# Smaller modulation transfers sent one by one, V's mix moved into an earlier call, and reordered seams, in a two-network transformer kernel

## The chip, the cores and the metric

The kernel runs on one core of a Trainium2 chip. The metric is the device time of one execution in microseconds (us). Before the change three runs took 2808.93 us in the median (2806.24 to 2821.59).

## The reference

The reference computes two networks on 256 rows of 1024 numbers, all in float32. Both have two layers.

```python
def first_block(x, ...):
    for layer in range(2):
        x = x + 0.5 * swiglu_ffn(rms_norm(x, ffn1_norm[layer]), w_gu, w_down)   # 1024 -> 2816 -> 1024
        p = rms_norm(x, mix_norm[layer]) @ w_in            # two gates, u_a, v_a, and r, k, v, low-rank parts
        y_a = chunked_sgu(u_a, v_a, ...)
        y_b, v_first = rwkv7_time_mix(token_shift_mix(p_b, mu), v_first, ...)
        x = x + (sigmoid(gate_a) * (y_a @ w_a) + sigmoid(gate_b) * (y_b @ w_b)) @ w_out
        x = x + 0.5 * swiglu_ffn(rms_norm(x, ffn2_norm[layer]), ...)
    return rms_norm(x, final_norm)

# inside rwkv7_time_mix, in the second layer alone:
v = v + (v_first - v) * sigmoid(v0 + v_res_down @ v2)

def second_block(x, c, ctx, ...):
    for i in range(2):
        sh1, sc1, g1, sh2, sc2, g2 = split(silu(c) @ ada_w[i] + ada_b[i], 6)    # "modulation"
        y = attention(rmsnorm(x) * (1 + sc1) + sh1, ctx ...)
        x = x + g1 * y
        x = x + g2 * conv_ffn(rmsnorm(x) * (1 + sc2) + sh2, ...)  # the context alike, in layer 0 only
    return rmsnorm(x, norm_out)
```

## The kernel before

**Weights.** All large weights come as one stream of 371 units of 1 MB each (128 rows of 2048 float32), in the order of use. SyncE sends unit u into `raw[u % 2]`. ScalarE copies it in a rounded type to `w_hi` (L1072), VectorE computes the rest `w_lo = raw - w_hi` (L1575), and both lie in 4 slots. A slot of `raw` is free for SyncE when `w_lo` is done, a slot of `w_hi`/`w_lo` when TensorE has used it (`unit_done`). The helper `split(n)` on ScalarE and on VectorE does this for the next n units, at places written by hand. Each product is three matmuls (`w_hi` by the feature's high part, `w_lo` by it, `w_hi` by the feature's low part), 24 for a unit.

**Engines.** Each engine has its own program, in order, and they meet in semaphores. `Side` keeps the counts. A normalised feature is made so: TensorE transposes X into a bank of PSUM (`raw_half`, `normed_features`), VectorE scales it to `TF`, ScalarE copies `TF` to `HA_hi`, VectorE forms `HA_lo`. In the first network this needs no norm, as the rows' rates are applied to the product later (`raw_features`). In the second (`modulated`) the rates come first: squares and a square root on ScalarE, a diagonal matrix on VectorE (`DIAG`), a matmul that spreads it over the partitions, then `TF`.

**The first network's mixer.** After 14 units (`pb`) come low-rank products, and then `wkv(l, g, t)` four times in each layer: `wkv_parallel` builds products of keys and inverts 64x64 triangles in five levels (`TM` on VectorE, two matmul groups, `XX` on ScalarE), and `wkv_chain` carries the state over two chunks. TensorE's instructions here are thousands of 64x64 matmuls, written out without a loop.

**Modulation.** The 24 MB of `ada_w` of each layer are brought in 24 units during this stage into `ADW`, which has 8 slots on the memory of `w_hi` and `w_lo`. SyncE sends unit n as soon as slot n-8 has been used (`ada_used`, L404). TensorE uses four units at each of the four calls, the first eight ahead of them (`mod_units`). Behind these 24 issues in SyncE's queue stands the next unit of the weight stream (L387). In layer 1 the two slots of `raw` hold `VF` and `VSIG` for V's mix, so the stream also waits for `v_ready`.

**V's mix** (`v_residual(t)`, layer 1): three VectorE instructions for rows t=0 ahead of the calls, and three for t=1 at the start of the second call, (g, t) = (0, 1).

**Seams.** A seam is a place where one stage's end must be normalised before the next stage can start: `mixer_residual` and `ffn_residual` with `raw_features` in the first network, `attend` and `conv_ffn` in the second, and the last norm and output. `down()` multiplies by the down-projection with both pairs of PSUM banks, `ACC[0]` and `ACC[1]`.

Of the kernel before, what the change touches and what calls it, by code (L numbers as in the profile page):

```python
# [131 lines left out]
PB_END = [PLAN[f"gate_a{l}"][0] for l in range(2)]  # L132

# [53 lines left out]
def build(nc, wstream, wada, vecs, cols, consts, x_in, ctx_in, mus, lora, lort, wst, convw, cc, lam,  # L187
          toe, rope, window, out, mod_scr, vfirst_scr):
    ctx = ExitStack()
    with ctx:  # L190
# [189 lines left out]
        def _(eng):  # L380
            for u in range(RAW):
                eng.dma_start(raw[:, u, :], wstream[u]).then_inc(sem[f"land{u}"], 16)
# [14 lines left out]

            def modulation(l):
# [14 lines left out]
            eng.wait_ge(sem["out_ready"], 1)  # L413
            eng.dma_start(out.rearrange("a (t p) d -> p (a t) d", p=P), XN[:, :, :]).then_inc(sem["out_land"], 16)
            eng.wait_ge(sem["out_land"], 16)
# [3 lines left out]
        def _(pe):  # L419
# [245 lines left out]
            def mod_units(l, a, b):  # L665

                for n in range(a, b):
                    group, k = divmod(n, 8)
                    bank = MOD_BANK[group]
                    pe.wait_ge(sem[f"ada_land{n % ADA_SLOTS}"], c.next(f"ada_land{n % ADA_SLOTS}", 16))  # L670
# [266 lines left out]
            def attend():  # L937
# [14 lines left out]
                for j in range(2):  # L952
                    block_wide(HA_hi, HA_lo)

            def conv_ffn(l, s):
                if l:
                    normed_features(X, 0)
# [30 lines left out]
            for l in range(2):  # L988
                project(l)
                if l:  # L990
                    attend()
                    phase()
# [4 lines left out]
            phase()  # L997
# [58 lines left out]
        def _(act):  # L1056
# [26 lines left out]

            def root(n, dst=None, at=0):
# [55 lines left out]
            def swiglu(first=False, last=False):  # L1140
                raw_features(0 if first else 1)
# [306 lines left out]
            def attend():  # L1448
# [26 lines left out]
                for j in range(2):  # L1475
                    e.skip(2, 1)
                    split(2)

            def conv_ffn(l, s):
                if l:  # L1480
                    row_squares(0)
                    modulated(1, 1, 0)
                else:
# [53 lines left out]

            act.wait_ge(sem["const_land"], c.next("const_land", 32))
            split(2)
# [7 lines left out]
            for l in range(2):  # L1547
                project(l)
                if l:
                    attend()  # L1550
                    phase()
# [4 lines left out]
            phase()  # L1556
            squares(X, XN)
# [3 lines left out]
        def _(dve):  # L1561
# [89 lines left out]
            def raw_features(gain, residual=None):  # L1651

                for h in range(2):
                    if residual:
                        residual(h)
                    raw_half(gain, h)
                if residual:
                    split(2)
                dve.wait_ge(sem["ss_ready"], c.next("ss_ready"))
# [52 lines left out]
            def mixer_residual(n):  # L1712

                x = cols(X, n)
                dve.wait_ge(sem["unit_done"], e.reached())
# [3 lines left out]
                if n == 0:  # L1719
                    split(2)  # L1720
# [32 lines left out]
            def v_residual(t):  # L1753

                tt(VF[:, t, :], VF[:, t, :], V[:, t, :], ALU.subtract)
                dve.drain()
                tt(VF[:, t, :], VF[:, t, :], VSIG[:, t, :], ALU.mult)
                dve.drain()
                tt(V[:, t, :], V[:, t, :], VF[:, t, :], ALU.add)
                dve.drain()  # L1760
# [786 lines left out]
```

## Time and profile before

| | |
|---|---|
| profiled execution | 2815.72 us, span 2813.8 us |
| TensorE (PE) busy | 2641.3 us, 94% of the span |
| weight loads (PEld) | 2113.4 us, 75% |
| VectorE (DVE) / ScalarE (ACT) | 1691.4 us, 60% / 1399.0 us, 50% |
| DMA | 477.80 MB, mean 170 GB/s |
| granted clock of TensorE | 0.971 of full speed, mean |

Busy time of TensorE is modelled and can hide short stops; the chain of work that ended last tells more. In a row, `L430` is the helper of all matmuls, `L506` that of the transposes, "issue" is time in which an engine waited for nothing that the profile shows. `SPq` is SyncE's queue.

### The profile page before, as it was taken

Reading aid. Unit: us, or ns where it says so; the run is one execution under the profiler, and the core shown is the slowest. Engines: PE = TensorE matmul, PEld = TensorE weight load, DVE = VectorE, ACT = ScalarE, POOL = GpSimd, SP = SyncE. Lnnn points to the kernel's source line nnn. Section 1 sums busy time; section 2 is a strip of 40 time slices with the busy share of each in tenths; the row PEclk is TensorE's granted clock in tenths of the full one; section 3 lists DMA queues with packets and bytes.
Section 4 is the critical chain, followed back from the end, with each engine's and each line's share of the span. In section 5 each row is a group of like instructions: output and inputs, shape, how many; then the busy total and the mean of one; then the engine's idle time right before and its main releaser. Section 6 shows DMA issues by size and latency. Waiting matters only on the chain.

```text
span 2813.8 us, 45474 instructions
## 1 busy us (share of the span) xinstructions
PE 2641.3 (94%) x18123; PEld 2113.4 (75%) x18123; DVE 1691.4 (60%) x1882; ACT 1399.0 (50%) x1679; POOL 78.3 (3%) x109
## 2 busy tenths in 40 slices
PE   6999888999999999888999999988999999997998
PEld 5877576887878877567878887757888887866886
DVE  4545735765545546646755555677776776455574
ACT  4435333644434434334536444474775764455573
POOL 0001000000000001000000000000000000010000
PEclk9999998999999999999999999999999999988999
DMA  4556922444454458532554544403544454523343
GB/s 186 193 187 234 369 81 85 170 175 179 179 194 178 181 186 291 232 127 99 195 190 179 195 174 155 165 1 115 196 177 175 175 193 163 190 88 125 120 179 120
DMA packets 73419, 477.80 MB, mean 170 GB/s; under 512 B 8830, under 2 KB 13020, under 8 KB 18864
## 3 DMA queue, kind: packets, MB, share of 16 engines
q1 hardware_dynamic: 60608, 440.43, 41.9%
q0 software_dynamic: 8048, 30.93, 3.1%
q10 hardware_dynamic: 4608, 4.20, 0.6%
q8 instruction: 120, 1.97, 0.3%
q14 instruction: 35, 0.29, 0.0%
HBM read 466.83 MB, written 2.13 MB: 167 GB/s over the span
## 4 chain that ended last, share of the span: by engine, by line
PE 81%; DVE 7%; DMA 4%; ACT 4%; issue 2%; DVEq 1%; ACTq 0%; POOL 0%; SPq 0%; POOLq 0%
PE ACC L430 72%; PE TP L506 3%; PE MM L430 3%; DMA raw<-wstream 3%; DVE w_lo L1575 2%; PE TP L430 2%; ACT w_hi L1072 1%; DMA ADW<-wada 1%; DVE ST L2060 1%; PE TP L882 1%; ACT XX L1214 1%; DMA BIAS<-toe 0%; DVE PR L2072 0%; DMA COL<-cols 0%; ACT U L1228 0%
## 5 line engine op out<-in xcount | busy, mean ns | idle before, releaser
L1575 DVE TENSOR_TENSOR w_lo<-raw,w_hi 128x2048 fp32r<-128x2048 f32 x371 | 842.0, 2290 | 383.6 <-ACT w_hi L1072 360.9
L1072 ACT ACTIVATE w_hi<-raw 128x2048 fp32r<-128x2048 f32 x371 | 703.9, 1916 | 413.4 <-DMA raw<-wstream 271.8
L430 PE MATMUL ACC<-w_hi,HA_hi 128*128 128x512 f32 (+1 forms) x2032 | 807.3, 397 | 31.8 <-DVE HA_lo L1647 13.9
L430 PE MATMUL ACC<-w_hi,HA_lo 128*128 128x512 f32 (+1 forms) x2032 | 796.0, 392 | 0.0
L430 PE MATMUL ACC<-w_lo,HA_hi 128*128 128x512 f32 (+1 forms) x2032 | 796.0, 392 | 0.0
L430 PEld LDWEIGHTS ACC<-w_hi,HA_hi 128*128 128x128 f32 x2032 | 387.8, 191 | 115.9 <-issue 25.9
L430 PEld LDWEIGHTS ACC<-w_hi,HA_lo 128*128 128x128 f32 x2032 | 387.3, 191 | 81.1
L430 PEld LDWEIGHTS ACC<-w_lo,HA_hi 128*128 128x128 f32 x2032 | 388.2, 191 | 76.5
L430 PE MATMUL ACC<-w_hi,FT_hi 128*128 128x512 f32 x616 | 246.0, 399 | 7.0 <-issue 7.0
L430 PE MATMUL ACC<-w_hi,FT_lo 128*128 128x512 f32 x616 | 244.2, 396 | 0.0
L430 PE MATMUL ACC<-w_lo,FT_hi 128*128 128x512 f32 x616 | 244.1, 396 | 0.0
L1149 ACT ACTIVATE HID<-ACC,ST 128x256 f32<-128x256 f32 x88 | 37.0, 471 | 221.7 <-PE ACC L430 221.7
L430 PEld LDWEIGHTS ACC<-w_hi,FT_hi 128*128 128x128 f32 x616 | 116.0, 188 | 35.6 <-issue 8.4
L1674 DVE SCALAR_TENSOR_TENSOR HID<-ACC,ST,HID 128x256 f32<-128x256 f32 x88 | 38.6, 480 | 168.1 <-ACT HID L1149 168.1
L430 PEld LDWEIGHTS ACC<-w_hi,FT_lo 128*128 128x128 f32 x616 | 116.0, 188 | 28.2
L430 PEld LDWEIGHTS ACC<-w_lo,FT_hi 128*128 128x128 f32 x616 | 116.1, 188 | 27.3
L430 PE MATMUL ACC<-w_hi,HB_hi 128*128 128x512 f32 x320 | 128.3, 401 | 0.1
L430 PE MATMUL ACC<-w_hi,HB_lo 128*128 128x512 f32 x320 | 126.8, 396 | 0.0
L430 PE MATMUL ACC<-w_lo,HB_hi 128*128 128x512 f32 x320 | 126.8, 396 | 0.0
L2242 DVE SCALAR_TENSOR_TENSOR CV<-TP,CW,CV 128x255 f32<-128x255 f32 x132 | 57.6, 478 | 67.5 <-ACT CV L1501 58.2
L430 PEld LDWEIGHTS MM<-VV,AT 128*128 128x128 f32 x448 | 61.0, 213 | 38.2 <-issue 30.3
L430 PE MATMUL MM<-VV,AT 128*128 128x64 f32 (+1 forms) x448 | 68.8, 306 | 7.2 <-ACT AT L1394 6.3
(333 smaller groups left out, 2855.4 us busy)
## 6 DMA issues: line engine op xcount, KB each, us to landing
raw<-wstream SPq DMA_DIRECT2D x371, 1024.0 KB, 4.8
ADW<-wada SPq DMA_DIRECT2D x48, 1024.0 KB, 10.7
BC<-vecs POOLq DMA_DIRECT2D x16, 512.0 KB, 6.3
BIAS<-toe ACTq DMA_DIRECT2D x32, 128.0 KB, 2.8
BC<-mod_scr POOLq DMA_DIRECT2D x6, 512.0 KB, 4.4
WA<-lora POOLq DMA_DIRECT2D x2, 1024.0 KB, 14.4
PREV<-R POOLq DMA_DIRECT2D x4, 448.0 KB, 5.5
PREV<-K POOLq DMA_DIRECT2D x4, 448.0 KB, 5.7
```

The costliest lines, as they stand in the source:

```text
L430: return pe.matmul(*a, skip_group_check=True, **k)
L506: last = pe.transpose(bank[:, (NT * k + t) * P:(NT * k + t + 1) * P], src[:, t, (k0 + k) * P:(k0 + k + 1) * P], ident())
L882: last = pe.transpose(TP[st["tp"] % 2][:, P * k:P * k + P], (PRB if heads_ == 2 else PR)[:, n % 2, hb, P * k:P * k + P], ident())
L1072: act.activation(w_hi[:, s, :], unit, ACT.Copy).then_inc(sem["hi_ready"], 1)
L1149: last = act.activation(HID[:, b % 2, t, :], acc[:, t, 0:256], ACT.Silu, scale=RN[:, t:t + 1])
L1214: act.activation(XX[:, 4 * h:4 * h + 4, :, :].rearrange("p n a x -> p a n x"), INV[h][:, :, 0:256].rearrange("p a (n x) -> p a n x", n=4), ...
L1575: dve.tensor_tensor(w_lo[:, s, :], unit, w_hi[:, s, :].bitcast(F32), ALU.subtract).then_inc(sem["lo_ready"], 1)
L1674: last = stt(h, acc[:, t, 256:512], RN[:, t:t + 1], h, ALU.mult, ALU.mult)
L2060: dve.tensor_reduce(ST[:, st0 + 2:st0 + 4], ACC[(n + e.z) % 2][:, :, 0:w], AX.X, ALU.max, negate=True) \
L2242: stt(y[:, 1:T], u[:, 0:T - 1], CW[:, 0, col], y[:, 1:T], ALU.mult, ALU.add)
```

## The change

1. `modulation(l)`: units 10 to 23 of each layer are sent as two transfers of 512 KB each. Each of them waits until the transfer before it has landed, the first of unit 10 for unit 9.
2. `v_residual(1)`: its three instructions stand in the first call, one behind `TM` of each of the levels 0, 1 and 2.
3. The start: SyncE sends the second weight unit when X has landed. ScalarE and VectorE split unit 0 before they wait for the constants, VectorE splits unit 1 between the halves of the first features, and `lam_sums` stands behind these.
4. `raw_features` on ScalarE: the two units are split behind the first two feature groups (one ahead of each pair of groups before). `mixer_residual` on VectorE: one unit between its first half and the features, the other ahead of its second half.
5. `mixer` on VectorE: the wait for `mu_land` stands behind the first two units.
6. `down()` on TensorE: the first unit is taken bank pair by bank pair, and the second pair is waited for only then.
7. From the second layer's attention to its `conv_ffn`, and at the end: squares are taken half by half (`half_squares`, with the table of the square root loaded in between), the rates follow as `left_rates` and `half_rates`, X's first half is turned during the last product block, VectorE's `split(2)` stands behind the features, and the `phase` barriers of all engines are gone. The output goes as two transfers.

```diff
+ADA_WHOLE = 10
+def ada_parts(n):
+    return 1 if n < ADA_WHOLE else 2
...
             for u in range(RAW):
+                if u:
+                    eng.wait_ge(sem["x_land"], 16)
                 eng.dma_start(raw[:, u, :], wstream[u]).then_inc(sem[f"land{u}"], 16)
...
-                    eng.dma_start(ADW[:, ada_slot(l, n), :], wada[ADA_UNITS * l + n]) \
-                        .then_inc(sem[f"ada_land{n % ADA_SLOTS}"], 16)
+                    parts = ada_parts(n)
+                    for k in range(parts):
+                        if parts > 1:
+                            before = (n if k else n - 1) % ADA_SLOTS
+                            eng.wait_ge(sem[f"ada_land{before}"], landed[before])
+                        w = UNIT // parts
+                        eng.dma_start(ADW[:, ada_slot(l, n), w * k:w * k + w],
+                                      wada[ADA_UNITS * l + n][:, w * k:w * k + w]) \
+                            .then_inc(sem[f"ada_land{n % ADA_SLOTS}"], 16)
+                        landed[n % ADA_SLOTS] += 16
...
             def down(mid=None):
-                for n in range(2):
-                    pe.wait_ge(sem[f"acc_free{(st['b'] + n) % 2}"], c.next(f"acc_free{(st['b'] + n) % 2}"))
                 for j in range(FT // 2 - 2):
                     pe.wait_ge(sem["feat_ready"], c.next("feat_ready"))
                     pe.wait_ge(sem["lo_ready"], c.next("lo_ready"))
-                    for k in range(2):
-                        for n in range(2):
+                    for n in range(2):
+                        if j == 0:
+                            pe.wait_ge(sem[f"acc_free{(st['b'] + n) % 2}"], c.next(f"acc_free{(st['b'] + n) % 2}"))
+                        for k in range(2):
                             last = down_part(j, k, n)
...
+            def half_squares():
+                for h in range(2):
+                    act.wait_ge(sem["x_half"], c.next("x_half"))
+                    act.drain()
+                    for t in range(NT):
+                        last = act.activation(JUNK[:, 512 * t:512 * t + 512], X[:, t, 512 * h:512 * h + 512], ACT.Square,
+                                              accum_out=SS[:, 2 * h + t:2 * h + t + 1])
+                    last.then_inc(sem["ss_ready"], 1)
+                    if h == 0:
+                        act.drain()
+                        act.activation(JUNK[:, 0:1], SS[:, 0:1], ACT.Sqrt)
+                root(2)
...
-            def raw_features(late=1):
+            def raw_features(late=2):
                 e.skip_turns(4)
                 for g in range(KT // 2):
-                    if g % 2 == 0:
-                        split(late)
                     act.wait_ge(sem["tf_ready"], c.next("tf_ready"))
                     act.activation(HA_hi[:, 2 * g:2 * g + 2, :].rearrange("p k n -> p (k n)"), TF[:, g % 2, :],
                                    ACT.Copy).then_inc(sem["hi_feat"], 1)
+                    if g == 1:
+                        split(late)
...
             def mixer_residual(n):
                 x = cols(X, n)
+                if n:
+                    split(1)
                 dve.wait_ge(sem["unit_done"], e.reached())
...
                 if n == 0:
-                    split(2)
+                    split(1)
...
-                    if l:
-                        v_residual(1)
-                        dve.drain().then_inc(sem["v_ready"], 1)
...
+                    if l and (g, t) == (0, 0) and j < 3:
+                        v_residual(1, (j,))
+                        if j == 2:
+                            dve.drain().then_inc(sem["v_ready"], 1)
...
+            def left_rates():
+                dve.wait_ge(sem["ss_ready"], c.next("ss_ready"))
+                ts(RS[:, 2:4], SS[:, 0:2], 1.0 / D, NORM_EPS, ALU.mult, ALU.add)
+
+            def half_rates():
+                dve.wait_ge(sem["ss_ready"], c.next("ss_ready"))
+                stt(RS[:, 0:2], SS[:, 2:4], 1.0 / D, RS[:, 2:4], ALU.mult, ALU.add)
+                dve.drain()
+                dve.reciprocal(RS[:, 0:2], RS[:, 0:2]).then_inc(sem["rs_pre"], 1)
+                dve.wait_ge(sem["rs_ready"], c.next("rs_ready"))
...
-            scaled_rows(v, "out")
-            dve.drain().then_inc(sem["out_ready"], 1)
+            half_rates()
+            for t in range(NT):
+                stt(XN[:, t, :], X[:, t, :], RS[:, t:t + 1], v, ALU.mult, ALU.mult).then_inc(sem["out_ready"], 1)
```

VectorE's order between the last attention product and the second layer's `conv_ffn`, before the change. `XN` and `X` are the gated residual's two steps, `RS` the rates, `HA_lo` the features' low part:

```order
L2208 TENSOR_TENSOR XN<-ACC,BC 128x2x512
L2211 TENSOR_TENSOR X<-X,XN 128x2x512
L1575 TENSOR_TENSOR w_lo<-raw,w_hi 128x2048 x2
L1603 TENSOR_SCALAR RS<-SS 128x2
L1607 RECIPROCAL RS<-RS 128x2
L2013 TENSOR_SCALAR DIAG<-K__58,RS 128x128 x2
```

And the same place after the change:

```order
L2267 TENSOR_TENSOR XN<-ACC,BC 128x2x512
L2270 TENSOR_TENSOR X<-X,XN 128x2x512
L2087 SCALAR_TENSOR_TENSOR RS<-SS,RS 128x2
L2089 RECIPROCAL RS<-RS 128x2
L2056 TENSOR_SCALAR DIAG<-K__58,RS 128x128 x2
```

The two weight splits have gone from between the residual and the rates; they stand behind the last `HA_lo`, where the row reads `w_lo<-raw,w_hi` x4.

SyncE's order at the eleventh modulation unit, as the change has it (`ADW` is the modulation buffer):

```order
L422 DMA ADW<-wada 128x2048 [waits unit_done] x8
L422 DMA ADW<-wada 128x2048 [waits ada_used] x2
L422 DMA ADW<-wada 128x1024 [waits ada_land1,ada_used]
L422 DMA ADW<-wada 128x1024 [waits ada_land2]
L422 DMA ADW<-wada 128x1024 [waits ada_land2,ada_used]
```

Before, the last three rows and those behind them were one: sixteen whole units that waited for `ada_used` alone.

## Rows read from the trace of the kernel before

**Rows 1.** The page, chain that ended last: share of the span by engine.

```profile
PE 81%; DVE 7%; DMA 4%; ACT 4%; issue 2%; DVEq 1%; ACTq 0%; POOL 0%; SPq 0%; POOLq 0%
```

**Rows 2.** The chain in order of time, start: start us, us, what.

```profile
3.14 9.81 DMA COL<-cols
...
14.91 2.29 DVE w_lo L1575
...
23.50 4.59 PE ACC L430 x12
```

**Rows 3.** Timeline of TensorE, two starts of `down()`: start, us, instruction, [idle before <-releaser].

```profile
781.04 0.47 PE L430 MATMUL ACC<-w_hi,FT_hi 128*128 128x512 f32 x1 [1.49 <-issue]
...
2096.42 0.47 PE L430 MATMUL ACC<-w_hi,FT_hi 128*128 128x512 f32 x1 [0.32 <-issue]
```

**Rows 4.** Timeline, from the mixer to the second feed-forward, layers 0 and 1.

```profile
643.09 2.29 DVE L1575 TENSOR_TENSOR w_lo<-raw,w_hi 128x2048 fp32r<-128x2048 f32 x1 [0.15 <-ACT w_hi L1072]
...
647.85 1.91 ACT L1072 ACTIVATE w_hi<-raw 128x2048 fp32r<-128x2048 f32 x1 [4.79 <-DMA raw<-wstream]
...
651.90 0.77 PE L430 MATMUL ACC<-w_hi,HA_hi 128*128 128x512 f32 x1 [3.12 <-issue]
...
660.37 0.50 PE L430 MATMUL ACC<-w_hi,HA_hi 128*128 128x512 f32 x1 [0.42 <-DVE HA_lo L1647]
...
1472.20 0.47 PE L430 MATMUL ACC<-w_hi,HA_hi 128*128 128x512 f32 x1 [2.59 <-issue]
```

**Rows 5.** Timeline of VectorE, start of the mixer, layer 0.

```profile
237.13 2.29 DVE L1575 TENSOR_TENSOR w_lo<-raw,w_hi 128x2048 fp32r<-128x2048 f32 x1 [8.38 <-DMA MU<-mus]
```

**Rows 6.** VectorE's `TM` at four levels, and a stretch: PE, PEld, DVE, ACT, POOL busy, clock, DMA.

```profile
351.08 0.42 DVE L1853 TENSOR_TENSOR TM<-ACC,K__58 128x256 f32<-128x256 f32 x1 [4.30 <-PE ACC L430]
...
357.20 0.42 DVE L1853 TENSOR_TENSOR TM<-ACC,K__58 128x256 f32<-128x256 f32 x1 [1.64 <-PE ACC L430]
...
386.46 0.42 DVE L1853 TENSOR_TENSOR TM<-ACC,K__58 128x256 f32<-128x256 f32 x1 [4.75 <-PE ACC L430]
...
1179.43 0.42 DVE L1853 TENSOR_TENSOR TM<-ACC,K__58 128x256 f32<-128x256 f32 x1 [3.14 <-PE ACC L430]
...
345.00:350.00 5.00, 2.75 (x125) 2.39 (x114) 0.85 (x2) 1.66 (x3) 0.00 (x0) 1.00 1.00 415
```

**Rows 7.** VectorE from the first call to the second, layers 0 and 1.

```profile
371.22 0.43 DVE L1867 TENSOR_TENSOR S<-ST_NEW,SG 128x256 f32<-128x256 f32 x1
...
376.78 1.29 DVE L1842 TENSOR_TENSOR LG<-MM,K__58 128x512 f32<-128x512 f32 x2 [0.58 <-PE MM L430]
...
1196.27 0.43 DVE L1867 TENSOR_TENSOR S<-ST_NEW,SG 128x256 f32<-128x256 f32 x1
...
1204.68 1.29 DVE L1842 TENSOR_TENSOR LG<-MM,K__58 128x512 f32<-128x512 f32 x2 [0.29 <-PE MM L430]
```

**Rows 8.** Layer 1: landing of units 9 and 10 (sent from 1134.1), of unit 18; stream, `w_hi`.

```profile
DMA to landing us min/median/max: 8.4/9.7/11.1
...
DMA to landing us min/median/max: 4.8/4.8/4.8
...
1229.73 0.36 SPq L387 DMA_DIRECT2D raw<-wstream  x1
...
1248.52 1.90 ACT L1072 ACTIVATE w_hi<-raw 128x2048 fp32r<-128x2048 f32 x1
```

**Rows 9.** The chain in order of time, from the last attention product to `conv_ffn`.

```profile
2589.27 2.20 DVE w_lo L1575
...
2596.46 1.28 ACT L1087
...
2605.32 24.64 PE ACC L430 x96
```

**Rows 10.** Timeline of the end.

```profile
2801.54 1.22 DVE L2211 TENSOR_TENSOR X<-X,XN 128x1024 f32<-128x1024 f32 x1
...
2809.42 0.41 SPq L414 DMA_DIRECT2D out<-XN  x1
```

More of the change, by code:

```diff
@@ L951, in attend @@
                 need_features()
-                for j in range(2):
-                    block_wide(HA_hi, HA_lo)
+                c.next("x_half", 2)
+                block_wide(HA_hi, HA_lo)
+                block_wide(HA_hi, HA_lo, between=lambda: raw_half(0))
             def conv_ffn(l, s):
                 if l:
-                    normed_features(X, 0)
+                    row_rates(0)
+                    raw_half(1)
                 def turn_up(b):
@@ L1140, in swiglu @@
             def swiglu(first=False, last=False):
-                raw_features(0 if first else 1)
+                raw_features(1 if first else 2)
                 if first:
@@ L1474, in attend @@
                 split(2)
-                for j in range(2):
-                    e.skip(2, 1)
-                    split(2)
+                e.skip(2, 1)
+                split(2)
+                half_squares()
+                e.skip(2, 1)
             def conv_ffn(l, s):
                 if l:
-                    row_squares(0)
                     modulated(1, 1, 0)
+                    split(2)
                 else:
@@ L1656, in raw_features @@
                     raw_half(gain, h)
+                    if h == 0 and not residual:
+                        split(1)
                 if residual:
                     split(2)
+                else:
+                    lam_sums()
                 dve.wait_ge(sem["ss_ready"], c.next("ss_ready"))
@@ L1751, in prepare, with v_residual @@
                 dve.drain().then_inc(sem["keys_ready"], 1)
[L1753 to L1760, printed above, removed]
+            def v_residual(t, steps=range(3)):
+                for step in steps:
+                    if step < 2:
+                        tt(VF[:, t, :], VF[:, t, :], (V, VSIG)[step][:, t, :], (ALU.subtract, ALU.mult)[step])
+                    else:
+                        tt(V[:, t, :], V[:, t, :], VF[:, t, :], ALU.add)
+                    dve.drain()
             def scaled_keys(t):
@@ L1909, in mixer @@
                 raw_features(G_MIX + 8 * l, ffn_residual)
-                dve.wait_ge(sem["mu_land"], c.next("mu_land", 16))
                 for n in range(7):
@@ L1914, in mixer @@
                         split(2)
+                    if n == 0:
+                        dve.wait_ge(sem["mu_land"], c.next("mu_land", 16))
                     if l == 0 and n == 2:
@@ L1995, in mixer, with scaled_rows @@
                 split(2)
-            def scaled_rows(v, name):
-                if name is not None:
-                    dve.drain().then_inc(sem["res_ready"], 1)
+            def scaled_rows(v):
                 dve.wait_ge(sem["ss_ready"], c.next("ss_ready"))
@@ L2004, in scaled_rows, with row_rates @@
                 for t in range(NT):
-                    stt((X if name is None else XN)[:, t, :], X[:, t, :], RS[:, t:t + 1], v, ALU.mult, ALU.mult)
-            def row_rates(s, first=False):
-                dve.wait_ge(sem["ss_ready"], c.next("ss_ready"))
-                rates(2, D, NORM_EPS, at=2 * s)
-                dve.wait_ge(sem["rs_ready"], c.next("rs_ready"))
+                    stt(X[:, t, :], X[:, t, :], RS[:, t:t + 1], v, ALU.mult, ALU.mult)
+            def row_rates(s, first=False, halves=False):
+                if halves:
+                    half_rates()
+                else:
+                    dve.wait_ge(sem["ss_ready"], c.next("ss_ready"))
+                    rates(2, D, NORM_EPS, at=2 * s)
+                    dve.wait_ge(sem["rs_ready"], c.next("rs_ready"))
                 for t in range(NT):
@@ L2202, in attend @@
                     gated(e.pair(), g, j, X)
-                    split(2)
+                    dve.drain().then_inc(sem["x_half"], 1)
+                    if j == 0:
+                        split(2)
+                        left_rates()
                 dve.drain().then_inc(sem["bc_free"], 1)
@@ L2227, in conv_ffn @@
                 if l:
-                    dve.drain().then_inc(sem["norm_ready"], 1)
-                    modulated(l, 1, s)
+                    row_rates(s, halves=True)
+                    modulated_part(l, 1, s, range(KT // 2))
+                    split(2)
                 else:
@@ L2293, in conv_ffn @@
                 split(2)
+            split(1)
             dve.wait_ge(sem["const_land"], c.next("const_land", 32))
@@ L2297, in _ @@
             dve.drain().then_inc(sem["x_half"], 2)
-            split(2)
-            lam_sums()
             for l in range(2):
```

35 lines of the change are left out of this document (19 added, 16 removed).

## The prediction

> **What bounds the kernel now.** I read the page's chain of waits first: 81% of the span is TensorE's own work, and DMA, VectorE, ScalarE and "issue" share the rest [rows 1]. So the change, which takes no matmul away, can only win what TensorE waits at certain places. I then read the chain in order of time and the timeline around each place that the change touches: the start [rows 2], the starts of `down()` [rows 3], the seams [rows 4, 9, 10] and the `wkv` calls [rows 6, 7]. Last comes SyncE's queue, since the change makes it wait more [rows 8].
>
> **The start.** The constants land at 3.1 + 9.8 = 12.95 us, and until then the DMA engines are full; at full load they carry 415 GB/s [rows 2, 6], so 1 MB takes 2.5 us of them. With the second weight unit held back the constants land near 10.4. Before, VectorE's two `w_lo` began at 14.91 and ended about 19.4, the first matmul came at 23.50 [rows 2]; with `lam_sums` (about 0.6 us) that leaves some 3.5 us for the features. Now unit 0 alone is split ahead of them: it is sent at about 1 us, lands in 4.8 (the page's median for the stream), and the table load (1.3), `w_hi` (1.9) and `w_lo` (2.3) end near 11.2. Features 3.5 us later: first matmul near 14.8, 8.7 us earlier. Unit 1, sent at about 8.5, lands at 13.3 and is split by 18, while TensorE needs it 8 us after its first matmul. I take 8.0; bounds 2.5 (only the megabyte) and 9.
>
> **`down()`.** Its first matmul waits 1.49 us in each of four feed-forwards of the first network, and 0.32 in each of three of the second [rows 3], for the bank pair that the last product has just filled. Now the other pair goes first, with 12 matmuls, 2.7 us, so the pair is free when its turn comes: 4 x 1.49 + 3 x 0.32 = 6.9 us. Nothing else is late next, the first unit's `w_lo` being two units ahead. Bounds 4 and 7.
>
> **From the mixer to the second feed-forward.** VectorE splits two units before the features, and ScalarE's `w_hi` at 647.85, which waits 4.79 us for its transfer, stands ahead of `HA_hi`: TensorE stops for 3.12 us, and 2.59 in layer 1 [rows 4]. With one `w_lo` (2.3 us) behind the features and `HA_hi` ahead of the splits these stops go. But the moved `w_lo` frees its slot of `raw` at about 648.9 instead of 645.4, the transfer lands 4.8 later, `w_hi` ends at 655.6, and behind it in ScalarE's queue stands the third group of `HA_hi`. The matmul of 660.37 [rows 4] then comes at about 657.7. The gain is 2.7, not 3.1; the same working gives 0.8 in layer 1. I take 3.0 of the 3.5; bounds 0 and 5.7. The other three seams with this order gain 0.1 each, since there the features end with the product anyway; they count as nothing.
>
> **`mu_land`.** VectorE's `w_lo` at 237.13 has waited for it [rows 5]; its `w_hi` was done at 235.2. The 1.9 us are those of a stage limited by its transfers, where an earlier slot helps in part. I take 0.5; bounds 0 and 1.9.
>
> **The calls of layer 0: whole units against halves.** In a level VectorE is idle 1.64 us between two pairs of `TM`; in one level of the first call it is 4.30, in one of the second 4.75 [rows 6]. The extra 2.66 + 3.11 = 5.8 us are time in which TensorE has nothing to wait for by the profile ("issue"), and the DMA engines are busy all of it (share 1.00), or have just got three units. I read it as TensorE's instructions arriving late behind the queued modulation units. Halves keep at most 512 KB on the way, 1.3 us of the engines. I take 5.0 for layer 0; bounds 0 (and, below it, the late halves under the rivals) and 7, since smaller excesses stand in the next levels.
> The Trainium skill (DMA: Bandwidth & Descriptors, section "Queues, rings and completion order") says that each DMA engine takes turns between the queues it has work for, a packet at a time, and that refills of instructions have a queue of their own. By that rule a long line of modulation units would not hold a refill up, and these 5 us would stay: the sum would be 2779. The rows speak against it so far, but they show stops beside load, not a cause.
>
> **The calls of layer 1.** From `S` to the second pair of `LG` the step to the second call takes 376.78 - 371.22 = 5.56 us in layer 0 and 1204.68 - 1196.27 = 8.41 in layer 1 [rows 7]; the difference of 2.85 is V's mix. In the levels its steps (1.23 each, with the drain 1.3) fit the idle 1.64. Late instructions add two excesses of 1.5 (3.14 against 1.64 [rows 6]). Against these 5 to 6 us stands SyncE's queue. Unit 9 lands at 1134.1 + 8.4 = 1142.5, and from there 27 halves must land before the last can be sent. A whole unit alone takes 4.8 [rows 8]; 1.3 less for half the bytes makes 3.5, and 0.1 to the next issue: 27 x 3.6 = 97, so the last half goes at 1239.7 instead of 1229.3. The stream's next unit is behind it in the queue, against 1229.73 before, and lands at about 1240.1 + 4.8 + 1.3 = 1246.2. ScalarE took it at 1248.52 [rows 8], and would now want it between 1243 and 1246. So the stream caps this layer at about 3 us. I take 3.0; bounds 6 (the halves faster than thought) and the late case below.
> The Trainium skill has (DMA: Bandwidth & Descriptors, section "Anatomy of one DMA — SWDGE (gpsimd) path") 2.0 us plus the bytes over 436 GB/s: 3.2 us for a half as an estimate, the cap gone and the sum 2 us lower. No row here shows a half.
>
> **To `conv_ffn` of layer 1.** Between the residual and the rates stand two `w_lo` of 2.20 and a table load of 1.28, and the squares over whole rows; TensorE's next product starts at 2605.32, 18.6 us after the last [rows 9]. Gone from this path are 4.4 + 1.28, about 0.9 of squares (half the columns) less small drains: 6.3. Added are eight transposes in the last product, 0.9. Net 5.4; bounds 3 and 6.5. The two units split later are needed 12 us after the features, and their splitting takes 4.5.
>
> **The end.** The residual ends at 2802.76, the output is sent at 2809.42 [rows 10] and takes 4.0 (the page). Gone: barrier 0.3, table load 1.3, 0.9 of squares; the second row tile's scaling (1.2) runs beside the first transfer, whose half is shorter but has a second behind it. I take 2.8; bounds 1.5 and 4.
>
> **Sum.** 8.0 + 6.9 + 3.0 + 0.5 + 5.0 + 3.0 + 5.4 + 2.8 = 34.6 us. From the profiled execution's 2815.7 that makes 2781.1. That execution was 6.8 us above the median of the three runs; from the median, 2808.93, it is 2774.3, and that I forecast: 2774.
>
> **Rivals.**
> A. Splitting the modulation units frees no instruction. Then 5.0 of layer 0 stay and the rest stands: 2779. For it: the rule above, and the stop in layer 1 with little on the way. Against it: the two longest stops fall under the fullest queue. Chance 0.17.
> B. The seams give half back. What is moved behind the features (two `w_lo` at the second network's seam, one in the mixer's) or behind X (unit 1) delays a transfer that a later step in order waits for. The start, the mixer's seam, `conv_ffn`'s and the end hold 19.2 us; half is 9.6: 2784. For it: ScalarE's wait of 4.79 for its transfer in rows 4. Against it: the stream runs at half its capacity elsewhere. Chance 0.14.
> C. The halves are late: slower than before. If a half takes nearly as long as a whole unit alone, 4.8 + 0.1 [rows 8], 27 of them take 132: the last goes at 1275, the stream's next unit lands at 1281 and holds ScalarE and the third call back by some 36 us against 1245. In layer 0 units 16 to 23 would come about 20 late. With the 8 us of fetch and V's mix lost: 2774 + 36 + 20 + 8 = 2838. It decides from a half of 3.7 us on, and passes zero gain in sum near 4.3. Against it: nothing but the bytes differs between a half and a whole, and 2.5 us per megabyte are seen. Chance 0.04.
> D. The change does little of this, since the waits that I name are followed by others I haven't seen: 2800. Chance 0.03.
> The forecast's own case has 0.62, with 2766 to 2782.
>
> **How the numbers follow.** A measurement of this kernel tells changes over 0.5%, 14 us, from none. The forecast, A and B are all faster by more than that (below 2794.9); C is slower, D is within. With what may be mis-sized, and runs that spread by 15 us before: faster 0.91, same 0.05, slower 0.04. The range that leaves out two in ten goes from 2764, where all terms but the capped one reach their upper bounds in part, to 2790, past B.
>
> **What would show it.** In the profile after: the first product matmul near 15 us; no wait ahead of the first matmul of `down()`; `TM` in the first two calls of layer 0 every 2.6 to 3 us; V's three steps in the idle time of levels 0 to 2 without a longer level; SyncE's last modulation half of layer 1 about 97 us after unit 9's landing, and ScalarE's `w_hi` of the third call waiting at most 3 us for `raw`; 13 us instead of 18.6 ahead of `conv_ffn`; 10 to 11 us from the last product's end to the end. I am wrong if a half takes over 4 us, if the levels still stretch, or if TensorE's stops come back one step behind each seam.

## The result, and the profile after

| | before | after |
|---|---|---|
| median of the runs shown with the result | 2811.8 us (2806.2 to 2821.6, 6 runs) | 2784.9 us (2782.4 to 2793.4, 6 runs) |
| ratio, 95% interval | | 0.9910 (0.9898 to 0.9923) |
| profiled execution, span | 2815.7, 2813.8 us | 2782.4, 2780.4 us |
| TensorE busy, granted clock | 2641.3 us, 0.971 | 2627.5 us, 0.975 |

27 us less by the medians, 33 by the two profiled executions; forecast were 35, to 2774. The time lies in the range, 11 us above the forecast. The terms outside the calls came close to what was worked out, that of layer 0 came in its sum but not in its places; that of layer 1 came with the other sign.

The chain that ended last, page of the kernel after:

```profile
PE 81%; DMA 6%; DVE 6%; ACT 3%; issue 2%; DVEq 1%; POOL 0%; ACTq 0%; SPq 0%; POOLq 0%
```

DMA has gone from 4 to 6% [rows 1]: the new share is modulation halves, one behind the other. The start, in the chain of waits of after (start us, us, what):

```profile
3.14 7.72 DMA COL<-cols
...
12.98 2.80 issue
15.78 5.10 PE ACC L451 x12
```

The constants land at 10.9 us instead of 12.95 and the product begins at 15.78 instead of 23.50 [rows 2]. At 40 us the kernel is 7.2 us ahead. The 2.80 us of "issue" are the making of the features: TensorE's transposes end at 12.98, and VectorE's first two `HA_lo` end at 15.68, 0.1 us ahead of the product (timeline of VectorE):

```profile
14.20 1.48 DVE L1681 TENSOR_TENSOR HA_lo<-TF,HA_hi 128x512 fp32r<-128x512 f32 x2
```

`down()`: TensorE's groups between 145 and 2330 us, of before and then of after (busy us, mean ns | idle before it):

```profile
L430 PE MATMUL ACC<-w_hi,FT_hi 128*128 128x512 f32 x492 | 196.7, 400 | 6.6 <-issue 6.6
```
```profile
L451 PE MATMUL ACC<-w_hi,FT_hi 128*128 128x512 f32 x526 | 210.2, 400 | 0.0
```

The 6.6 us ahead of `down()`'s matmuls [rows 3] are gone to the last tenth. The counts differ since the window cuts the last of them at another place; over the whole kernel these groups have 616 matmuls each, with 7.0 and 0.0 us of idle time. From the mixer to the second feed-forward, the timelines of TensorE show one stop a layer:

```profile
635.24 0.50 PE L451 MATMUL ACC<-w_hi,HA_hi 128*128 128x512 f32 x1 [2.42 <-DVE HA_lo L1681]
...
1454.20 0.79 PE L451 MATMUL ACC<-w_hi,HA_hi 128*128 128x512 f32 x1 [2.42 <-DVE HA_lo L1681]
```

The stops of 3.12 and 2.59 [rows 4] have gone and one of 2.42 stands a step later, as the prediction had it. What that gains is the whole seam's length: in layer 0 the matmul of 635.24 comes 20.9 us after VectorE began the residual's first half (614.34), and before 23.7 (636.71 to 660.37), so 2.8 us; by the same measure layer 1 gains 0.8. Ahead of the second layer's `conv_ffn`, and at the end, the chain of waits reads:

```profile
2558.26 5.48 PE ACC L451 x24
...
2571.89 2.04 PE TP L527 x8
2573.93 1.90 issue
2575.82 4.61 PE ACC L451 x10
```
```profile
2770.99 1.23 DVE X L2270
...
2774.74 1.28 DVE XN L2385
```

From the last product's end at 2563.75 to the next product are 12.1 us instead of 18.6 [rows 9]; less 0.87 for eight transposes inside that product, 5.7 are gained. From the residual's end (2772.22) to the end of the span are 8.2 us instead of 11.0 [rows 10].

Then the calls. V's mix has found its place: VectorE's timeline, first call of layer 1, and the step to the second:

```profile
1142.62 0.42 DVE L1890 TENSOR_TENSOR TM<-ACC,K__58 128x256 f32<-128x256 f32 x1 [1.72 <-PE ACC L451]
...
1143.44 1.22 DVE L1797 TENSOR_TENSOR VF<-VF,V 128x1024 f32<-128x1024 f32 x1
...
1164.91 0.43 DVE L1908 TENSOR_TENSOR S<-ST_NEW,SG 128x256 f32<-128x256 f32 x1
...
1170.48 1.29 DVE L1879 TENSOR_TENSOR LG<-MM,K__58 128x512 f32<-128x512 f32 x2 [0.58 <-PE MM L451]
...
1207.44 0.43 DVE L1890 TENSOR_TENSOR TM<-ACC,K__58 128x256 f32<-128x256 f32 x1 [1.84 <-PE ACC L451]
...
1254.24 0.43 DVE L1890 TENSOR_TENSOR TM<-ACC,K__58 128x256 f32<-128x256 f32 x1 [1.72 <-PE ACC L451]
```

`S` to the second `LG` takes 5.57 us, against 8.41 before and 5.56 in layer 0 [rows 7]. But from the third call's first `TM` to the fourth's are 46.8 us, where before it took 34.5. The reason, in the page's DMA issues (count, KB, median us to landing), in SyncE's timeline, in the chain, and in the waits of TensorE from 1100 to 1310 us (total, times, longest):

```profile
ADW<-wada SPq DMA_DIRECT2D x56, 512.0 KB, 3.8
```
```profile
1213.68 4.21 SPq L422 DMA_DIRECT2D ADW<-wada  x2
1217.99 0.46 SPq L397 DMA_DIRECT2D raw<-wstream  x1
```
```profile
1105.52 8.42 DMA ADW<-wada
...
1114.01 3.58 DMA ADW<-wada
...
1209.56 4.00 DMA ADW<-wada
1213.55 10.83 issue
1224.38 1.92 ACT w_hi L1093
```
```profile
PE ACC L451 <- ACT XX L1249: 12.6, 9, 10.7
```

From unit 9's landing at 1113.94 the halves follow each other back to back. ScalarE comes to the stream's unit at 1213.55, which SyncE sends only at 1217.99, behind the last half, and which is there at 1224.38. ScalarE's copy of `XX` stands behind that `w_hi`, and TensorE waits 10.7 us for `XX`. The row calls ScalarE's wait "issue", since the releaser is not seen; what ends it is shown by the experiments.

The call lost more than the wait, 12.3 us (34.5 to 46.8). While TensorE stood still its granted clock fell to the lower level, and it began again at that level (windows of TensorE, PEld, DVE, ACT, POOL busy, clock, DMA share, GB/s):

```profile
1220.00:1225.00 5.00, 0.00 (x0) 0.00 (x0) 0.00 (x0) 0.62 (x1) 0.00 (x0) 0.50 0.98 378
1225.00:1230.00 5.00, 2.97 (x68) 2.78 (x72) 3.67 (x4) 4.06 (x4) 0.00 (x0) 0.50 0.30 95
```

### The profile page after: what moved, and what is told of

Same layout as the page of the kernel before. It is cut to its first block, busy times and chain, and to the rows that moved or that the text cites. A ratio compares the mean times of both kernels' runs of the same rounds, so it can differ in the third digit from the quotient of the medians.

```text
span 2780.4 us, 45532 instructions
## 1 busy us (share of the span) xinstructions
PE 2627.5 (95%) x18123; PEld 2107.3 (76%) x18123; DVE 1692.4 (61%) x1884; ACT 1399.7 (50%) x1689; POOL 78.6 (3%) x109
## 4 chain that ended last, share of the span: by engine, by line
PE 81%; DMA 6%; DVE 6%; ACT 3%; issue 2%; DVEq 1%; POOL 0%; ACTq 0%; SPq 0%; POOLq 0%
PE ACC L451 73%; DMA ADW<-wada 4%; PE TP L527 3%; PE MM L451 3%; DMA raw<-wstream 2%; DVE w_lo L1609 1%; PE TP L451 1%; ACT w_hi L1093 1%; PE TP L903 1%; DVE ST L2116 1%; DMA PREV<-V 0%; DVE PR L2128 0%; DVE HA_lo L1681 0%; DMA BIAS<-toe 0%; ACT XX L1249 0%
## 5 line engine op out<-in xcount | busy, mean ns | idle before, releaser
L451 PEld LDWEIGHTS MM<-VV,AT 128*128 128x128 f32 x448 | 61.5, 215 | 39.3 <-issue 30.4
## 6 DMA issues: line engine op xcount, KB each, us to landing
ADW<-wada SPq DMA_DIRECT2D x20, 1024.0 KB, 12.1
```

Of the source, the lines that this page charges most:

```text
L451: return pe.matmul(*a, skip_group_check=True, **k)
```

## The experiments

For the calls one measure tells more than the total: from VectorE's first `TM` of call 1 to its first `TM` of call 4, in us of each profile.

| kernel | layer 0 | layer 1 | median us (runs) | ratio to before, 95% |
|---|---|---|---|---|
| before | 107.8 | 105.4 | 2811.8 (6) with after, 2811.9 (11) with e1 to e4, 2811.8 (21) with e5 to e8, 2809.4 (11) with e9 to e11 | |
| after | 102.9 | 111.6 | 2784.9 (6) | 0.9898 to 0.9923 |
| e1_whole | 112.1 | 100.9 | 2778.1 (5) | 0.9861 to 0.9898 |
| e2_halves_layer0 | 102.8 | 103.3 | 2775.7 (5) | 0.9857 to 0.9887 |
| e3_early | 101.8 | 105.6 | 2775.4 (4) | 0.9847 to 0.9882 |
| e4_halves_unchained | 107.3 | 101.6 | 2787.7 (6) | 0.9889 to 0.9920 |
| e5_whole_chained | 105.7 | 111.0 | 2784.4 (6) | 0.9877 to 0.9921 |
| e6_before_halves | 102.2 | 114.5 | 2811.4 (12) | 0.9993 to 1.0016 |
| e7_mix_back | 101.6 | 104.3 | 2773.7 (4) | 0.9838 to 0.9875 |
| e8_calls_only | 102.9 | 100.6 | 2803.4 (10) | 0.9960 to 0.9982 |
| e9_down_back | 101.8 | 102.7 | 2788.8 (6) | 0.9896 to 0.9937 |
| e10_stream_in_chain | 102.4 | 100.4 | 2774.5 (4) | 0.9861 to 0.9889 |
| e11_unit1_at_once | 101.9 | 101.6 | 2777.9 (4) | 0.9873 to 0.9904 |

My theory: halves sent one by one take away stops of TensorE, which I read as late instructions, but in layer 1 they stand in SyncE's queue ahead of the stream's unit. Rivals: the split frees nothing; the third call stops for another reason.

**Whole units again.**

```diff
-ADA_WHOLE = 10
+ADA_WHOLE = 24
```

> The changed kernel (2784.9 us median, profiled execution 2782.4) with all modulation units whole again; V's mix, seams, start and down() stay. Theory: halves take away stops of TensorE for late instructions in the first two calls of each layer, but in layer 1 they stand in SyncE's queue ahead of the stream's unit and stop the third call for 10.8 us. Then here the third call of layer 1 stops for less than 2 us, the stops of 2 to 3 us in a level of the first two calls come back (5 to 6 us in layer 0, 3 in layer 1), and the time is about the same or a little less: 2779 to 2785. Rival (the split takes no stop away): the levels stay as they are, only the 10.8 us come back: 2774.

The third call's stop goes (layer 1: 100.9), and the levels of layer 0 stretch again (VectorE's timeline, first call):

```profile
338.55 0.42 DVE L1890 TENSOR_TENSOR TM<-ACC,K__58 128x256 f32<-128x256 f32 x1 [1.97 <-PE ACC L451]
...
343.79 0.42 DVE L1890 TENSOR_TENSOR TM<-ACC,K__58 128x256 f32<-128x256 f32 x1 [4.34 <-PE ACC L451]
```

5.2 us for a level that takes 2.6 in after. So halves sent one by one do take the stops of the first call away; rival A is out. That the stops are instructions which arrive late stays an inference: no row shows one arriving. Of layer 0's 112.1 some 6 are another thing: its third call took 41.4 us against 35.2 in e4. TensorE ran at half speed there, 16 `MM` matmuls in 1.12 us where before took 0.68 (timelines of TensorE, e1 and before, and a window of e1 with the granted clock of 0.50):

```profile
430.77 1.12 PE L451 MATMUL MM<-S,ABT 64*64 64x64 f32 x16 [0.17 <-DVE S L1908]
```
```profile
438.41 0.68 PE L430 MATMUL MM<-S,ABT 64*64 64x64 f32 x16 [0.56 <-DVE S L1867]
```
```profile
430.00:435.00 5.00, 4.83 (x80) 4.46 (x76) 2.16 (x6) 0.97 (x2) 0.00 (x0) 0.50 0.01 3
```

The median is 2778.1, a little under the range expected: whole units in both layers are 6.7 us better than halves in both.

**Halves in layer 0 only.**

```diff
-    return 1 if n < ADA_WHOLE else 2
+    return 1 if l or n < ADA_WHOLE else 2
```

> Halves in layer 0 only, whole units in layer 1, all else as changed. Theory: layer 0 keeps its levels of 2.6 us in the first call; layer 1 wins the 10.8 us of the third call and loses 3 of them to late instructions: 2777. Rival (the third call's stop comes from something else than the halves in SyncE's queue): it stays at about 10 us and the time is 2785 or more.

2775.7, as expected, 9.2 below the change; the intervals of the two ratios don't meet.

**The stream's next two units ahead of the last modulation units.**

```diff
                         landed[n % ADA_SLOTS] += 16
+                    if l and n == 17:
+                        eng.wait_ge(sem["v_ready"], 1)
+                        for u in range(PB_END[1], PB_END[1] + RAW):
+                            eng.wait_ge(sem["lo_ready"], u + 1 - RAW)
+                            eng.dma_start(raw[:, u % RAW, :], wstream[u]).then_inc(sem[f"land{u % RAW}"], 16)
```

> All as changed, but in layer 1 SyncE waits for V's mix and sends the stream's next two units behind modulation unit 17 instead of behind unit 23. Theory (the place in SyncE's queue is the cause of the third call's 10.8 us): ScalarE's w_hi in the third call does not wait for raw, and the time is 9 to 11 us less, 2775; the last modulation units land up to 5 us later, which none waits for. Rival (the DMA engines or the modulation units themselves are late in the third call): TensorE then waits for ADW in the third or fourth call for about as long, 2783 to 2787.

The same halves, another place in the queue. ScalarE's timeline, third call:

```profile
1221.60 1.91 ACT L1097 ACTIVATE w_hi<-raw 128x2048 fp32r<-128x2048 f32 x1
```

No wait ahead of it, and 2775.4 us. That shows the cause of the 10.8 us: the stream's unit is sent behind the halves. A new stop came in the second call, with the two units on the way (its level takes 5.4 us; 2.6 in after, 4.2 in e1 and e2):

```profile
1186.85 0.42 DVE L1894 TENSOR_TENSOR TM<-ACC,K__58 128x256 f32<-128x256 f32 x1 [4.47 <-PE ACC L455]
```

**Size without order, and order without size.** In the first both halves are sent at once; in the second whole units wait for each other.

```diff
-                            eng.wait_ge(sem[f"ada_land{before}"], landed[before])
```
```diff
-ADA_WHOLE = 10
+ADA_WHOLE = 24
...
-                        if parts > 1:
+                        if n >= 10:
```

> Halves as changed, but sent without waiting for the landing of the transfer before: the size alone. If the size of a transfer is what delays TensorE's instructions, the levels of layer 0 stay at 2.6 us and the third call of layer 1 has no stop: 2775. If it is how much is queued at once, the stops of 2 to 3 us in the first two calls come back as with whole units, and the third call's stop goes: 2779 to 2785, like the run with whole units.

> The changed kernel with whole modulation units from the eleventh on, each sent only when the one before has landed: the ordering without the smaller size. Measure: from VectorE's first TM of call 1 to its first TM of call 4. Layer 0 took 107.8 us before, 102 to 103 with halves one by one, 107 to 112 with whole units or halves sent without waiting. Theory (what counts is how much is queued at once, and 1 MB is little enough): layer 0 at 102 to 104; a whole unit alone takes about 5 us where two halves take 7.7, so SyncE gets to the stream's unit 25 us sooner, no stop in the third call of layer 1 (100 to 103 us against 111.6), and 2774 us. Rival (512 KB is what it takes): layer 0 at 107 or more, 2779.

Halves without waiting behave as whole units: 107.3 in layer 0, with this row in the first call:

```profile
342.50 0.42 DVE L1890 TENSOR_TENSOR TM<-ACC,K__58 128x256 f32<-128x256 f32 x1 [4.77 <-PE ACC L451]
```

The size alone gives nothing in layer 0. Whole units one by one take 105.7 there, and TensorE stops with a single megabyte on the way (chain of waits):

```profile
341.90 2.50 issue
344.40 0.87 PE TP L451 x27
```

I had expected 102 to 104, and 100 to 103 in layer 1, which took 111.0 with no wait for the stream in its third call: the first two took 37.1 and 39.3 us instead of 31.9 and 32.9. The third call blurs layer 0, since before and e1 have a fallen clock in it. The first two calls alone take 66.3 to 68.3 us in the nine profiles with halves one by one, 70.7 in e5, and 70.7 to 72.0 in before, e1 and e4. So it takes both, 512 KB and one at a time; neither alone shows a gain. The median of the unchained halves, 2787.7, is 2.8 above after's, while their two spans are 5.6 shorter in sum; what else they cost is open. Both kernels came out slower than any theory or rival had them, and only the spans tell these apart.

**The halves alone, in the kernel before** (the `ada_parts` and `modulation` parts of the change and nothing else).

> The kernel before with the modulation units as the change sends them (halves one by one from the eleventh on), and nothing else. Theory: from call 1 to call 4 layer 0 takes 102 to 103 us instead of 107.8; layer 1, with the slower first calls of the kernel before, gets its stream's unit 5 to 8 us late and takes 108 to 111 instead of 105.4; in sum nothing, 2808 to 2814. Rival (splitting is worth what the prediction gave it, 5 us in layer 0 and some in layer 1): 2804 or less.

Nothing by the medians, 2811.4 against 2811.8. By the spans 5.6 are gained in layer 0 and 9.1 lost in layer 1, which at 114.5 is past the 108 to 111 that I had expected; a loss of 3.5 in sum is not seen in the time. Its chain shows the same stop without any other part of the change:

```profile
1243.48 9.73 issue
1253.22 1.92 ACT w_hi L1090
```

**V's mix back in the second call** (halves in layer 0 only; the three steps stand ahead of the second call's grams again).

> Halves in layer 0 only, and V's mix for the second row tile back in the second call of layer 1, all else as changed. Theory: the mix costs its 2.9 us ahead of the second call again, in layer 1 from call 1 to call 4 106 us instead of 103.4, the time 2779. Rival (it is hidden in the second call anyway, the gain of layer 1 came from timely instructions): 103 us and 2776.

From the first call's first `TM` to the second's are 35.7 us against 31.7, and over the three steps 104.3. The five kernels with the mix moved, whole units in layer 1 and nothing else at work there (e1, e2, e8, e9, e11) have 100.6 to 103.3, 101.8 in the mean. So by the traces the move gains 4.0 us up to the second call, but over the three steps only 2.5 against the mean of the five, and 1.0 against e2, its nearest kernel, whose second call is slower. The times, 2773.7 and 2775.7, show no gain at all: the intervals overlap, and the kernel with the mix put back has the lower median.

**The calls' parts alone** (the kernel before with halves in layer 0 and the mix moved).

> The kernel before with two parts alone: halves in layer 0 and V's mix in the first call. No change of the start, the seams, down() and the end. Theory: the two parts are worth 5 and 3 us and the rest 26.6 as predicted: 2775.7 + 26.6 = 2802. Rival (half of the seams' gain is taken back by transfers that come later): 2790 to 2796.

2803.4. Of what is gained up to e2, 36.1 us, the calls hold 8.4 and start, seams, `down()` and end hold 27.7; predicted were 5.0 + 3.0 and 26.6. Rival B, half of the seams' gain given back, is out: it would have left 17.0.

**`down()` in the old order** (halves in layer 0 only; the two waits ahead of the loop, and `for k` around `for n`).

> Halves in layer 0 only (2775.7 us median), with the first unit of down() taken in the order of the kernel before, both bank pairs waited for at once. Theory: TensorE stops 1.49 us ahead of the first matmul of down() in four feed-forwards and 0.32 in three again, 6.9 us in all: 2782 to 2783. Rival (the features or the transfers of the next units are late right behind anyway): the stops show, but at most 3 us are lost, 2778.

TensorE's groups from 145 to 2330 us:

```profile
L451 PE MATMUL ACC<-w_hi,FT_hi 128*128 128x512 f32 x504 | 201.5, 400 | 6.6 <-issue 6.6
```

The stops are back with the 6.6 us they had. The median rose by 13.1, though, which the stops do not explain. Aligned by equal instructions, e9's profile is 0.8 us ahead of e2's at the start and 12.9 behind at the end; beyond the stops some 7 us are lost in stretches whose code is equal. Part of it goes with the granted clock: the three longest runs, 2790.9 to 2794.6, have 0.973 and 0.974, the shortest, 2776.6, has 0.980, and e2's five have 0.975 to 0.980. What the rest is stays open.

**The stream in the chain** (both layers in halves; unit 155 behind modulation unit 15 and unit 156 behind 19, each alone on the way).

```diff
+                    if l and n in (15, 19):
+                        u = PB_END[1] + (n == 19)
...
+                        eng.wait_ge(sem[f"ada_land{n % ADA_SLOTS}"], landed[n % ADA_SLOTS])
+                        eng.dma_start(raw[:, u % RAW, :], wstream[u]).then_inc(sem[f"land{u % RAW}"], 16)
+                        eng.wait_ge(sem[f"land{u % RAW}"], 16 * (u // RAW + 1))
```

> Halves in both layers as changed, and in layer 1 the stream's next two units in the same line: one behind modulation unit 15, one behind unit 19, each sent when the half before has landed, and the next half when it has. With two units sent at once behind unit 17 the second call had a stop of 2.7 us more in a level (1181.5 to 1186.8), with 2 MB on the way. Theory (late instructions come with 1 MB and more on the way): a single 1 MB may cost one stop of up to 2.5 us, the third call has none for raw, layer 1 takes 101 to 104 us from call 1 to call 4, and the time is 2772 to 2775, the lowest of all. Rival (the stops in layer 1 have nothing to do with what is on the way): they stay at 105 us, as with the stream's units sent together, 2776 or more.

100.4 us in layer 1 from the first of these rows to the second, the least of all, and 2774.5 us:

```profile
1150.97 0.43 DVE L1896 TENSOR_TENSOR TM<-ACC,K__58 128x256 f32<-128x256 f32 x1 [1.72 <-PE ACC L457]
...
1251.34 0.42 DVE L1896 TENSOR_TENSOR TM<-ACC,K__58 128x256 f32<-128x256 f32 x1 [1.72 <-PE ACC L457]
```

Against e3, where the two units went together, it is 5.2 us less. Against whole units in layer 1 (101.8 in the mean) it is hardly anything. This, e2, e3 and e7 are all below before and after, and cannot be told from each other.

**The second unit sent at once** (halves in layer 0 only, the wait for `x_land` gone).

> Halves in layer 0 only, with the second weight unit sent at once again instead of when X has landed; the order on VectorE and ScalarE at the start stays as changed. Theory: the constants land 2.5 us later for the megabyte ahead of them, and the first matmul of the first product comes at 18.3 instead of 15.8 us: 2778. Rival (the order of the work, not the megabyte, gave the whole of the start's gain): the first matmul stays within 1 us of 15.8 and the time at 2776.

```profile
3.13 9.61 DMA COL<-cols
...
14.87 2.80 issue
17.67 5.11 PE ACC L449 x12
```

The constants land 1.9 us later than in after and the product follows by 1.9 (2.5 were expected): the megabyte is worth about 2 of the start's 7.2 us, the order on the engines the rest. The medians, 2777.9 and 2775.7, cannot tell e11 from e2.

## Why the prediction was right in its direction, and where it failed

The step that failed is the term "The calls of layer 1", +3.0. Between the `TM`s the layer lost 6.2 us (105.4 to 111.6), and by medians splitting it costs 9.2 (e2 against after). What was mis-sized in it is the step of the chain of halves, set at 3.6 us and measured at 3.85. Its parts:

- V's mix, 2.85: measured 5.57 instead of 8.41 to the second call, so 2.84. Right in its place; by e7 between 1.0 and 2.5 of it are left over three calls, and nothing shows in the time.
- V's mix and late instructions together: the first two calls took 64.8 us instead of 70.9, 6.1 less, when "5 to 6" was expected. Right.
- The halves: 3.6 us each was the estimate, 97 for 27, and the stream's issue 97.6 after unit 9's landing. The interval from that landing at 1113.94 to the stream's issue at 1217.99 is 104.1, 3.85 each. That is 6.5 us late, and a half took 3.8, past the 3.7 from which rival C was said to decide. The estimate took 1.3 us off a whole unit for half the bytes; measured, half the bytes saved 1.0 (4.8 to 3.8). A quarter of a microsecond in a step that is repeated 27 times makes 6.5 of the 10.8 us, and the bounds "6 and the late case" had no price between them.
- The cap itself: ScalarE had the unit 6.4 us after its issue (6.1 predicted), and wanted it 99.6 us after unit 9's landing, where the prediction had room until 100.5 to 103.5. That makes the other 4 of the 10.8 us, of which the prediction had allowed up to 3. The mechanism was named and the queue's order was right; the margin was taken from a best guess where it should have had a range of its own.
- The granted clock had no term: behind the wait it was 0.50 until 1230, and the call lost 12.3 us instead of 10.8.

So rival C was half true: its mechanism came, in layer 1 only, at a third of its 36 us. In layer 0 the halves came in time, and no unit was waited for.

The Trainium skill (DMA: Bandwidth & Descriptors, "Anatomy of one DMA — SWDGE (gpsimd) path") makes a half 3.2 us by the formula that the prediction quoted, a fit to another path of issue than SyncE's; by that the cap would not have come. The median of 3.8 in after's profile decides against it here. By the Trainium skill (DMA: Bandwidth & Descriptors, "Queues, rings and completion order") a refill of instructions would pass a loaded queue. Here a level of the first call took 5.2 us with many units queued (before, e1) or 5.7 with unchained halves (e4), and 2.6 to 3.5 with halves one by one. So in the first call the load does make TensorE stop, but that a refill is what it waits for no row shows.

The other terms, predicted and measured: start 8.0 and 7.2; `down()` 6.9 and 6.6; mixer 3.0 and 3.6; layer 0 5.0 and 4.9; to `conv_ffn` 5.4 and 5.7; end 2.8 and 2.9. The start's path was another than the prediction had: it let the features follow unit 0's `w_lo`, which it set at 11.2 us, and gave them 3.5. The `w_lo` was done at 9.9, the constants landed at 10.9, and from there to the product are 4.9 us, as TensorE's transposes now stand in that path too. So the product came at 15.78, not 14.8.

In layer 0 the sum is right in part by luck. The first call gave 3.6 us (34.9 to 31.3 from its first `TM` to the next call's), and the third 1.8, which were not counted and which the halves need not have given: there before has a stop of 1.14 ("issue" in its chain, at 431.79) and behind it a granted clock of 0.81 to 0.85 until 440, and e4, with unchained halves, takes 35.2 against after's 34.9. In the eight other profiles with halves one by one the first two calls gain 2.8 to 4.8 us on before, in after 3.1. The second call, for which 3.11 were set, gave nothing in after (36.2 and 36.7) and 0.7 to 1.6 in those eight. Its stop stands where it stood, in the first level: VectorE is idle 3.84 us there instead of 4.75 [rows 6], and nothing is on the way (the chain of after, and the window 365.7 to 367.7 with a DMA share of 0.00):

```profile
365.78 1.86 issue
```
```profile
365.70:367.70 2.00, 0.14 (x5) 0.06 (x3) 0.00 (x0) 0.00 (x0) 0.00 (x0) 1.00 0.00 0
```

That level takes 3.7 to 4.7 us in all nine profiles with halves one by one, and 2.6 in e5. What makes TensorE late there is open; a full queue it is not. "If the levels still stretch" was a sign of being wrong, and in the second call they do.

For `mu_land` nothing can be told: the first `TM` of layer 0 came at 331.9 and 332.4 us in after and e5, but at 336.5 to 338.6 in e1 to e4, e7 and e10, with the same code up to there (345.2 to 345.9 in the three kernels with the old start). That spread of up to 6.7 us is larger than the term. Its cause is open. The profiled pair shows 33 us where the medians show 27 because before's profiled execution is 3.9 above its median and after's, one of the two early ones, 2.5 below. Last, the three runs that I started from had a median 2.9 us below that of later ones (2808.9, 2811.8), which takes the forecast from a level a little too low.

By medians the 27 us are 8.4 (calls, halves in layer 0 only) and 27.7 (the rest), less 9.2 (halves in layer 1). These are differences between e8, e2 and after in a row, so that they add up proves nothing; each is only as good as its two medians. The time lay in the range because the 9 us by which the layer 1 term was off (3.0 gained, 6.2 lost) are less than the range's 16 us above the forecast.

## What to carry to other kernels

A transfer that waits for the one before makes a chain whose length is count times duration: price it with a range, and look for what stands behind it in the same queue. If a part with a deadline is there, send it inside the chain (e10) or leave the chain out where its gain is small (e2). A change that acts in two places can win in one and lose in the other; by medians the halves alone sum to zero, so time each place by itself.

## What the runs showed of the hardware that was not expected

In the first call of layer 0 TensorE's stops go with what is on the way: with one 512 KB half at a time its levels take 10.5 to 12.2 us from the first `TM` to the fifth in nine profiles, with a single 1 MB unit 13.9 (e5), and much the same with many units (13.9 and 14.0) or unchained halves (14.2). In the second call the difference is small: 12.4 to 14.5 with halves one by one, 12.6 with whole units one by one, 13.9 to 14.8 with the others, and one stop stands there with nothing on the way.

In the second layer's attention (2440 to 2530 us) the granted clock fell, in after to 0.50, the lower level of 1.2 GHz. In e1's profile it did not fall there at all, in the twelve others for a part of that stretch, the longest in before and after. Windows of 10 us (PE, PEld, DVE, ACT, POOL busy, clock, DMA share, GB/s), of after and then of e1:

```profile
2450.00:2460.00 10.00, 8.11 (x33) 4.45 (x31) 7.32 (x9) 7.18 (x9) 0.00 (x0) 0.87 0.30 111
2460.00:2470.00 10.00, 10.00 (x34) 6.62 (x34) 6.85 (x17) 5.94 (x16) 2.54 (x2) 0.50 0.42 152
2470.00:2480.00 10.00, 10.00 (x43) 8.17 (x43) 5.20 (x13) 3.23 (x8) 2.02 (x2) 0.50 0.20 52
```
```profile
2460.00:2470.00 10.00, 7.26 (x35) 3.85 (x33) 8.28 (x11) 6.78 (x9) 0.00 (x0) 1.00 0.51 197
2470.00:2480.00 10.00, 7.72 (x54) 5.52 (x54) 7.03 (x18) 6.54 (x16) 2.54 (x2) 1.00 0.31 92
```

Both follow the same idle time of TensorE, of about 1.8 us; in after the fall begins right behind it (0.86 in 2456 to 2458, then 0.50), in e1 there is none. Aligned by equal instructions, e1 wins about 8 us on after in that stretch, with the same code. Before had the fall too (0.50 from 2490 to 2500), so the profiled pair is fair in this; but profiles of one execution each can differ by 8 us there and by 4 to 7 ahead of layer 0's calls, which is more than most terms of this change. Local rows, and not totals, told the terms apart.
